# The first stage of a two-block kernel: weight remainders on VectorE, the recurrence's root by logarithms, the first norm in another order

## The reference

```
sh1, sc1, ... = silu(c) @ ada_w + ada_b               # modulation, one row of weights per output column
h = rms_norm(x, norm_mix_g) * (1.0 + sc1) + sh1       # first norm
xr, gr, q, k, v = split(h @ ev_w_in, 5)               # each 512 wide
xr = causal_dwconv(xr, ev_conv_w, ev_conv_b)          # 4 taps
r, i = sigmoid(xr @ wa + ba), sigmoid(xr @ wx + bx)   # 8 diagonal blocks of 64
log_a = -8.0 * r * softplus(-lam)
a, u = exp(log_a), sqrt(-expm1(2.0 * log_a)) * (i * xr)
h_t = a_t * h_(t-1) + u_t                             # linear recurrence over the tokens
ya = h * gelu(gr)
q, k = rms_norm per head of 64
yb = stick_breaking(q, k, v)                          # attention, 8 heads
mix = concat([ya, yb]) @ ev_w_out
```

## Time and profile before

| | |
|---|---|
| median of 3 runs | 3756.47 us (3754.92 to 3760.41) |
| profiled execution | 3753.44 us |
| its span, first to last instruction | 3751.6 us |
| busy in the span: TensorE / VectorE / ScalarE / GpSimd | 3599.6 / 2019.4 / 1332.3 / 128.5 us |
| mean granted TensorE clock | 0.978 |
| chain that ended last | 85% TensorE, 11% VectorE |

### The profile page before, as it was taken

How to read it: one execution, slowest core, us unless ns; L and a number is a source line. 1 busy time by engine, 2 the same in 40 slices (tenths; PEclk the granted TensorE clock), 3 DMA queues, 4 the chain that set the end, 5 groups by cost and what they waited for, 6 DMA issues and landing times.

```text
span 3751.6 us, 41675 instructions
## 1 busy us (share of the span) xinstructions
PE 3599.6 (96%) x16712; PEld 2888.0 (77%) x16712; DVE 2019.4 (54%) x3608; ACT 1332.3 (36%) x2291; POOL 128.5 (3%) x126
## 2 busy tenths in 40 slices
PE   6899999999999999998999999999999999989998
PEld 5647888766888888885677888888878888868886
DVE  7856756576757654576765235523553333344233
ACT  3563323353423332234443223323324334333222
POOL 3330000000000000001100000000000000000000
PEclk9989999999999999999999999999999999989999
DMA  6314555422555455521012222222222222212231
GB/s 258 107 40 144 197 193 174 141 80 74 180 194 194 151 190 195 192 101 65 29 51 96 96 96 96 85 96 97 95 83 82 75 83 78 62 55 95 96 101 62
DMA packets 155469, 429.09 MB, mean 114 GB/s; under 512 B 45468, under 2 KB 50524, under 8 KB 155277
## 3 DMA queue, kind: packets, MB, share of 16 engines
q1 hardware_dynamic: 155276, 426.45, 33.5%
HBM read 423.98 MB, written 2.40 MB: 114 GB/s over the span
## 4 chain that ended last, share of the span: by engine, by line
PE 85%; DVE 11%; ACT 2%; issue 1%; DMA 0%; POOL 0%; SPq 0%; ACTq 0%; DVEq 0%; POOLq 0%
PE ps L420 25%; PE ps L421 24%; PE ps L422 24%; PE ps L731 1%; PE ps L457 1%; PE ps L711 1%; PE ps L771 1%; PE ps L809 1%; DVE X L1621 1%; DVE mraw L1456 1%; PE ps L796 1%; DVE HL L1520 1%; PE ps L577 1%; DVE TT L1535 1%; PE ps L470 1%
## 5 line engine op out<-in xcount | busy, mean ns | idle before, releaser
L420 PE MATMUL ps<-HH,whi 128*128 128x512 f32 x3168 | 1254.9, 396 | 26.1 <-DVE HL L1520 13.0
L421 PE MATMUL ps<-HL,whi 128*128 128x512 f32 x3168 | 1238.1, 391 | 0.0
L422 PE MATMUL ps<-HH,wlo 128*128 128x512 f32 x3168 | 1238.0, 391 | 0.0
L1468 DVE TENSOR_TENSOR wlo<-wraw,whi 128x1024 fp32r<-128x1024 f32 x526 | 644.1, 1225 | 774.2 <-ACT whi L934 774.0
L934 ACT ACTIVATE whi<-wraw 128x1024 fp32r<-128x1024 f32 x548 | 576.1, 1054 | 693.5 <-PE ps L422 684.6
L420 PEld LDWEIGHTS ps<-HH,whi 128*128 128x128 f32 x3168 | 597.8, 189 | 166.2 <-issue 35.8
L421 PEld LDWEIGHTS ps<-HL,whi 128*128 128x128 f32 x3168 | 597.9, 189 | 126.1 <-issue 4.9
L422 PEld LDWEIGHTS ps<-HH,wlo 128*128 128x128 f32 x3168 | 597.7, 189 | 126.2
L1456 DVE CUSTOM_DVE_ANT_0 mraw<-mraw,CB 128x1024 f32<-128x1024 f32 x224 | 282.3, 1262 | 0.9 <-DMA mraw<-mst 0.9
L1654 DVE TENSOR_TENSOR TT<-TT,ps 128x512 f32<-128x512 f32 x116 | 79.7, 687 | 212.9 <-PE ps L422 182.2
L420 PE MATMUL ps<-PHf,whi 128*128 128x512 f32 x352 | 136.9, 389 | 0.0
(11 more groups left out here) (327 smaller groups left out, 3928.4 us busy)
## 6 DMA issues: line engine op xcount, KB each, us to landing
wraw<-wst SPq DMA_DIRECT2D x548, 512.0 KB, 3.3
mraw<-mst SPq DMA_DIRECT2D x224, 512.0 KB, 4.3
MR<-mst SPq DMA_DIRECT2D x16, 512.0 KB, 13.8
X<-xt SPq DMA_DIRECT2D x8, 256.0 KB, 5.1
BB<-bvec SPq DMA_DIRECT2D x8, 256.0 KB, 3.4
TT<-lse SPq DMA_DIRECT2D x16, 128.0 KB, 3.0
out<-X SPq DMA_DIRECT2D x8, 256.0 KB, 2.0
CB<-crow SPq DMA_DIRECT2D x2, 512.0 KB, 4.6
```

The costliest lines, as they stand in the source:

```text
L420: e.matmul(o[key], wh, sh(k), start=k == 0, stop=False)
L421: e.matmul(o[key], wh, sl(k), start=False, stop=False)
L422: ins = e.matmul(o[key], wl, sh(k), start=False, stop=k == nk - 1)
L1468: e.tensor_tensor(wlo[:, x % RAW, :], wraw[:, x % RAW, :], whi[:, x % SPLIT, :].bitcast(F32), ALU.subtract).then_inc(*wlo_made.up(x))
```

## The change

Three things are changed, all before `stick`.

1. **Weight remainders.** GpSimd's 22 subtractions go; VectorE's `feed` does all of them, blocks 0 to 3 within the first norm, one behind each even b(m). The semaphore of GpSimd's remainders goes too.
2. **The root.** sqrt(2 * th / (th - 1)) was a reciprocal on VectorE and a square root on ScalarE. Now ScalarE takes two logarithms (`lru_logs`), VectorE one difference (`lru_power`), ScalarE the exponential of its half (`lru_root`); logarithm and exponential are in the table that the norms use. The four recurrences stand in steps 1, 2, 4 and 5 instead of 4 to 7, and the wait for the high part stands one step later (`lru_low`).
3. **The first norm.** The squares' sums stand ahead of the wait for V. Modulation steps 9 and 1 are done in the gaps of the inverse root. Gain and shift of each tile go to ScalarE (`first_gain`). The step pairs stand between b(m) and HL(m) or behind it. `unread` is 5 instead of 8 in this norm, and SyncE issues weight block 0 behind row 1 instead of row 0.

The diff, cut to its core:

```diff
+        LN = [at("LN%d" % i, ph + 73728 + 2048 * i, [P, S]) for i in range(2)]
...
+        lru_steps = (1, 2, 4, 5)
...
-        def lo_signal(b):
-            return wlo_pool if b < 22 else wlo_made
...
-                    lane.wait_ge(lo_signal(b), b)
+                    lane.wait_ge(wlo_made, b)
...
-            norm_total(("f", 0, 0))
+            norm_total(("f", 0, 0), 5)
...
-            def lru_end(step):
-                if step == 4:
-                    for m in range(4):
-                        lane.wait_ge(v_mix, ("z", m))
-                        e.activation(XC[:, m, :], XC[:, m, :], ACT.Sqrt).then_inc(*a_mix.up(("sqr", m)))
-                    table("natural_log_exp_and_others")
...
+            def lru_logs(m):
...
+                e.activation(LN[m % 2][:], XC[:, m, :], ACT.Ln, scale=-2.0).then_inc(*a_mix.up(("lnn", m)))
+                e.activation(XC[:, m, :], XC[:, m, :], ACT.Ln, bias=1.0, scale=-1.0).then_inc(*a_mix.up(("lnd", m)))
+
+            def lru_root(m):
+                lane.wait_ge(v_mix, ("d", m))
+                e.activation(XC[:, m, :], XC[:, m, :], ACT.Exp, scale=0.5).then_inc(*a_mix.up(("sqr", m)))
...
+                table("natural_log_exp_and_others")
+                feed(8)
+                lru_logs(0)
...
-                    lru_end(i)
+                    if i - 1 in lru_steps:
+                        lru_high(lru_steps.index(i - 1))
+                    if i in lru_steps:
+                        lru_root(lru_steps.index(i))
...
+                    if i + 2 in lru_steps:
+                        lru_logs(lru_steps.index(i + 2))
...
+            def first_gain(m):
+                lane.wait_ge(v_mod, "amb")
+                lane.wait_ge(v_mod, ("step", m))
+                e.activation(AM[:, 0, m:m + 1], MOD[:, 1, m:m + 1], ACT.Identity, bias=small[:, 8 + m:9 + m],
+                             scale=gain_of("mix_g", 0)[:, m:m + 1]).then_inc(*a_norm.up(("am0", m)))
+                e.activation(MOD[:, 0, m:m + 1], MOD[:, 0, m:m + 1], ACT.Identity, bias=col("ada_b", m)).then_inc(
+                    *a_norm.up(("shift", m)))
...
+            def split(b):
+                if b < nblocks:
+                    lane.wait_ge(whi_made, b)
+                    e.tensor_tensor(wlo[:, b % RAW, :], wraw[:, b % RAW, :], whi[:, b % SPLIT, :].bitcast(F32),
+                                    ALU.subtract).then_inc(*wlo_made.up(b))
...
-                    e.reciprocal(z, z).then_inc(*v_mix.up(("z1", m)))
...
+            def lru_power(m):
+                lane.wait_ge(a_mix, ("lnd", m))
+                e.scalar_tensor_tensor(XC[:, m, :], LN[m % 2][:], -160.0, XC[:, m, :], ALU.max, ALU.subtract).then_inc(
+                    *v_mix.up(("d", m)))
...
-            for b in range(22):
-                split(b)
-
...
-                if m % 2 == 0:
+                if m == 1:
+                    load(0)
+                elif m in (2, 4, 6):
                     load(m // 2)
```

More of the change, by code:

```diff
@@ L341, in program @@
         wlo_made = Signal(sem("wlo_made"))
-        wlo_pool = Signal(sem("wlo_pool"))
         a_norm = Signal(sem("a_norm"))
@@ L1400, in scalar_engine @@
             rsqrt(s, 4)
+            first_gain(0)
+            split(0)
+            first_gain(1)
             for m in range(8):
-                if m % 2 == 0 and m // 2 < SPLIT:
-                    split(m // 2)
-                lane.wait_ge(v_mod, ("shift", m))
+                lane.wait_ge(a_norm, ("shift", m))
                 lane.wait_ge(v_norm, ("b", s, m))
                 e.activation(HH[:, m, :], T[m % 5], ACT.Identity, bias=MOD[:, 0, m:m + 1]).then_inc(*a_norm.up(("hh", s, m)))
+                if m < 6:
+                    first_gain(m + 2)
+                    if m % 2 == 0:
+                        split(m // 2 + 1)
             e.activation(small[:, 0:4], col("lam", 0, 4), ACT.Abs).then_inc(*a_norm.up("lam0"))
@@ L1797, in even @@
                     feed(8)
-                    lru_end(i)
+                    if i - 1 in lru_steps:
+                        lru_low(lru_steps.index(i - 1))
+                    if i in lru_steps:
+                        lru_scan(lru_steps.index(i))
+                    if i + 1 in lru_steps:
+                        lru_power(lru_steps.index(i + 1))
                     if i:
@@ L2153, in vector_engine @@
             s, AMB = ("f", 0, 0), small[:, 8:16]
+            for m in range(8):
+                square_add(s, m)
             lane.wait_ge(vec_in, "vec")
             e.scalar_tensor_tensor(AMB, col("ada_b", 8, 8), 1.0, gain_of("mix_g", 0), ALU.add, ALU.mult).then_inc(*v_mod.up("amb"))
-            for m in range(8):
-                square_add(s, m)
             mod_step(8)
             mod_step(0)
+            lane.wait_ge(mm_done, ("toty", s))
+            half_of(s, total_of(("tot", s))[:, 0, :], tok[5])
+            mod_step(9)
+            rsqrt(s, 4)
+            freed[("tot", s)] = ((v_norm, ("r", s)),)
             lane.wait_ge(c_in["ident"], "in")
-            single(s)
-            lane.wait_ge(v_mod, "amb")
+            diagonal(s, 4, T[2])
+            mod_step(1)
             lane.wait_ge(mm_done, ("root", s))
@@ L2165, in vector_engine @@
             freed[("root", s)] = ((v_norm, ("b", s, 7)),)
-            def low(m):
+            for m in range(8):
+                if m >= 5:
+                    lane.wait_ge(v_norm, ("hl", s, m - 5))
+                lane.wait_ge(a_norm, ("am0", m))
+                e.scalar_tensor_tensor(T[m % 5], X[:, m, :], AM[:, 0, m:m + 1], R, ALU.mult, ALU.mult).then_inc(
+                    *v_norm.up(("b", s, m)))
+                if m % 2 == 0:
+                    split(m // 2)
+                elif m < 6:
+                    mod_step(10 + m)
                 lane.wait_ge(a_norm, ("hh", s, m))
@@ L2170, in low @@
                                        ALU.subtract).then_inc(*v_norm.up(("hl", s, m)))
-            for m in range(8):
-                if m:
-                    mod_step(8 + m)
-                    mod_step(m)
-                lane.wait_ge(v_mod, ("step", m))
-                e.scalar_tensor_tensor(AM[:, 0, m:m + 1], MOD[:, 1, m:m + 1], gain_of("mix_g", 0)[:, m:m + 1], AMB[:, m:m + 1],
-                                       ALU.mult, ALU.add).then_inc(*v_mod.up(("am", m)))
-                e.tensor_tensor(MOD[:, 0, m:m + 1], MOD[:, 0, m:m + 1], col("ada_b", m), ALU.add).then_inc(*v_mod.up(("shift", m)))
-                lane.wait_ge(v_mod, ("shift", m))
-                if m >= 5:
-                    lane.wait_ge(v_norm, ("hl", s, m - 5))
-                e.scalar_tensor_tensor(T[m % 5], X[:, m, :], AM[:, 0, m:m + 1], R, ALU.mult, ALU.mult).then_inc(
-                    *v_norm.up(("b", s, m)))
-                if m:
-                    low(m - 1)
-            low(7)
+                if m < 6:
+                    if m % 2 == 0:
+                        mod_step(10 + m)
+                    mod_step(2 + m)
             e.tensor_scalar(small[:, 4:8], col("lam", 0, 4), -1.0, 0.0, ALU.mult, ALU.max).then_inc(*v_mod.up("lam0"))
```

53 lines of the change are left out of this document (19 added, 34 removed).

## The result

The changed kernel takes a median of 3728.0 us (four runs, 3726.5 to 3731.5); the kernel before, measured beside it, 3755.7 (3753.5 to 3760.4). The ratio is 0.9924 with a 95% interval of 0.9909 to 0.9939: **27.7 us less**, where 25 were predicted, and 3728.0 lies in the range of 3725 to 3741. The profiled execution took 3727.55 us, with a span of 3725.8, which is 25.8 less than before.

The account below looks back on a forecast made before the run. VectorE was taken as the bound ahead of 66 us and behind 125 us, TensorE between. VectorE's ledger gave 27 us less, the path 26.6, cut to 25: 3753.4 became 3728.4, plus 3.0 for the median 3731 us, range 3725 to 3741.

Parts of the forecast that it names:

- The case forecast as likeliest: Whole stage before the attention: the path goes as priced, 25 us less, 3731 us; chance 0.58.
- the third case: Stage's end into the attention: the clock stays at 2.4 GHz, some 3 us more go, 3728 us; chance 0.13.
- The fourth rival: Long VectorE instructions stay long, their cause not being GpSimd; 3759 us, no change that shows; chance 0.05.
- My 34 us held: VectorE's time before the attention lost to GpSimd's 22 subtractions: about 34 us, 1.55 us per subtraction.
- Until b(0): Inverse root up to the first product: start from 26.8 to 20.1 us, 6.7 us sooner, bounds 19 and 23.
- First norm: From b(0) to the last HL: 35.9 to 31.1 us, ending at 51.2 instead of 62.7, 11.5 us sooner.
- Groups 2 and 3: Matmul groups behind the first norm: TensorE the bound, 52.8 us without a wait, ending at 106.8 us.
- Steps: Queries and keys: TensorE bounds by 2 us in 46, one wait of 1.7; attention at 162.7 instead of 189.31 us.
- VectorE standing at a weight remainder with ScalarE named: Sign in the changed kernel's profile that would show the prediction wrong: VectorE waiting there for ScalarE; no size given.
- the fifth rival: Steps of queries and keys: late weight copies make steps serial, 106 us instead of 54, 3783 us; chance 0.04.
- The additive ledger: VectorE's work before the attention: + 25.1 remainders, - 15.4 inversions, - 2.7 one-column operations, - 34 held time: 27 us less.
- TensorE waits in the steps: Steps of queries and keys: VectorE's slack is thin, each of eight costs 1 us; 17 us less, 3739; chance 0.20.

Follow-up runs that it names:

- part 1 alone: The kernel before with only GpSimd's 22 weight remainders moved to VectorE, root and first norm as before; median 3758.2 us, ratio 0.9994 to 1.0012 to the kernel before.
- part 1 undone: The changed kernel with GpSimd doing the remainders of blocks 0 to 21 again, root and norm as changed; median 3735.7 us.
- subtractions beside: The changed kernel plus two unread GpSimd subtractions of 384 columns at each of the first 22 weight copies; median 3754.0 us.
- fourteen operations more: The changed kernel plus two VectorE operations of 384 columns ahead of the norm in each of steps 1 to 7; median 3734.9 us.
- fills: The changed kernel plus two GpSimd fills of 384 columns at each of the first 22 weight copies; 3735.8 us in a single run, median 3723.9 us in five.
- three moves: The changed kernel with ScalarE's weight copies 14 and 15 earlier, remainder 0 before the root's wait, copies 1 to 3 behind the next HH; median 3724.5 us.

## Why the prediction was right, point by point

**The sum**: 25 us predicted, 27.7 measured, 25.8 between the two profiled executions. The case forecast as likeliest is the one that happened. The number alone can't say so: 3728.0 us is also what the third case (the clock comes back too) named, and only the windows rule that one out. And the end of the steps was met in part by luck, as shown below.

**The long instructions** are GpSimd's doing: shown by taking them away (part 1 alone), by keeping them (part 1 undone) and by bringing them back with other work (subtractions beside). The fourth rival, that they stay, fell. My 34 us held: part 1 alone moved the last gate 7.1 us ahead with 14 remainders more by then (16.0), and won 9.5 behind 118 us, 32.6 in all. Of the two rules weighed, the Trainium skill (SBUF — State Buffer, on the engine side's ports) counts two SBUF inputs of VectorE as enough for the lock against a GpSimd operation that reads SBUF. The traces agree on both sides of it: a remainder of 1.22 us takes 2.02 beside a subtraction, and 1.23 at most beside a fill, which reads nothing. The narrower rule of the Trainium skill (Advanced Engine Details and Errata, VectorE Performance Modes) names two-port instructions alone and doesn't cover these forms.

**Until b(0)**: predicted 20.1, measured 21.62, within the bounds of 19 and 23. The first step started at 14.26 for 13.5, and TensorE's spread of the root over the partitions took 2.08 us for 1.3 (1.12 before, where it came later, at 25.24 us), since TensorE still went at half its pace. Ten unread instructions ahead of the spread and fourteen behind it:

```profile
16.59 2.48 PE L463 MATMUL ps<-c_ones 128*128 128x128 f32 x10
...
21.37 1.77 PE L463 MATMUL ps<-c_ones 128*128 128x128 f32 x14
```

They start 0.21 and 0.11 us apart. The granted clock that the windows give here is 1.00 (18 to 20 us), so the lower level is read from this pace alone. In the other runs with this norm b(0) lay from 20.55 to 21.3.

**First norm**: 31.1 us forecast from b(0) to the end of the last `HL`, 31.3 measured (52.21 + 0.66 - 21.62), the waits for `HH` as forecast: 0.40 in the turns with a copy, 0.85 for the last. The gain and the shift take 0.39 and 0.28 us of ScalarE's time, where I took 0.2 from a form of four columns; it was covered.

**Groups 2 and 3**: 106.8 forecast, 106.73 measured; no remainder was late there. The last `HL` had come 1.7 us later than forecast (52.87 for 51.2) and the end of group 3 did not, so my way from the one to the other, 2.8 + 52.8, was 1.7 us too long.

**Steps**: the end was right (161.75 for 162.7) and the mechanism partly wrong. The forecast had TensorE as the bound with 2 us of slack for VectorE. It sized TensorE's step as 5.6 + 1.05, and it takes 6.34, 2.2 us less over seven; and it had one wait of 1.7 us, at the first norm, which didn't come, since the last gate that it hangs on was done 2.4 us sooner than forecast (104.44 for 106.8). The one wait there is, 0.3 us, stands at the seventh norm. So TensorE was through some 3 us sooner than the 160.7 of the forecast (157.7). The ledger of VectorE for the same steps left out the 7.2 us for which it stands at the copies of blocks 14 and 15, behind ScalarE's chain after the last gate: that chain was in my text, but only as a wait of TensorE's. The work itself was sized well: from the start of step 1 (117.57) to 161.6 VectorE takes 44.0 us, for 44.4 forecast. With the wait it starts step 1 so late that it ends last, as the fourteen operations more show by costing their full length. The two errors nearly cancelled, and that is luck. The prediction had named "VectorE standing at a weight remainder with ScalarE named" as a sign of being wrong; it came (9.6 us in all), and it was a sign of this error. VectorE's stand at the two remainders is the milder form of the fifth rival (VectorE queues behind ScalarE's copies): twice and not in each step.

**The additive ledger** was the weak part. It said + 25.1 - 15.4 - 2.7 - 34 and came out at 27, but its first and last term together, 9 us less, describe part 1, which by itself is worth 0, and 9.9 beside the others. It fits only because part 2 brings a wait for ScalarE at the same place anyway.

**The rivals.** TensorE waits in the steps: not seen (0.3 us). The clock comes back too: no, 0.50 from 170 to 180 us. Long instructions stay: no. Slower by chained engines: no; the copy is late by 3.17 and 4.01 us at blocks 14 and 15 (by 1.74 at block 10, where TensorE had work), and in time for every step after that.

## What to carry to other kernels

Price a moved operation at the place where it will stand, with what is queued behind it and what it waits for there: the same part was worth 0 us alone and 9.9 beside another that brought the same wait. Work given to an idle engine isn't free if it stretches the full one; look for one form with two durations (1.22 and 2.04 us) and for who is active during the long one. And where a total moves by less than a few tenths of a per cent, compare stations in the trace and time it several times: one run of 3735.8 us and five around 3723.9 were the same kernel, on two chips.

## What the runs showed of the hardware that was not expected

**One kernel differed by 17 us from one execution to another.** The one with fills ran six times, from 3718.9 to 3735.8 us. The slowest was alone on its chip and the five others on another, so the chip isn't ruled out as a cause; but the kernel before was the faster on the first of these chips (3754.2 for 3756.6), and ten runs of part 1 alone, all on one chip, lay 16 us apart as well (3749.8 to 3766.2). The two traced executions with fills are 0.7 us apart at the first update of X and 11.9 at the last. As differences to the changed kernel, at VectorE's first update of X in a layer:

| changed kernel, us | fills, single run | fills, one of five | three moves |
|---|---|---|---|
| 271.9 | -1.4 | -2.1 | -5.8 |
| 627.6 | -1.5 | -1.2 | -5.8 |
| 859.5 | +3.8 | -0.1 | -6.1 |
| 1941.9 | +10.2 | -0.1 | -1.8 |
| 2696.7 | +7.7 | -0.1 | -4.2 |
| 3712.9 | +8.2 | -3.7 | -3.5 |

Between 700 and 800 us the granted clock was 0.85 in the single run and 0.90 in the other three executions of the table. So the low stretches differ from one execution to another in code that is the same; that the small shifts of its start are the reason is my guess, and what makes the clock fall more in one execution wasn't found. The 1.8 us of this change that the two executions lose between the attention and the end are well within that.

**Which VectorE forms are held beside a GpSimd subtraction** shows in the kernel before, beside the three subtractions from 126.13 to 133.97 us:

```profile
126.85 2.56 DVE L1766 TENSOR_SCALAR TX<-XC 128x512 f32<-128x512 f32 x1
129.44 3.35 DVE L1768 RECIPROCAL TX<-TX 128x512 f32<-128x512 f32 x1
132.83 1.70 DVE L1770 SCALAR_TENSOR_TENSOR XC<-XC,TX 128x512 f32<-128x512 f32 x1
```

A subtraction of a scalar with one SBUF input, which takes 0.42 us for 512 columns when free, where the others take 0.69, took 2.56; the reciprocal, with one SBUF input too but 3.35 us long, was not held at all; the product of two SBUF tiles, 0.69 when free, took 1.70. And GpSimd pays as well: two subtractions of 384 columns took 2.08 us in all with VectorE seldom in its way (at 19.83 us), and six took 11.84 beside remainders and modulation steps.
